# One decoder layer on one core: two tile pairs' normalisation postponed, and five scan parts moved ahead of the attention slots

## The chip, the core and the metric

The kernel runs on one NeuronCore of a Trainium2 chip. TensorE (PE) multiplies, VectorE (DVE), ScalarE (ACT) and GpSimd (POOL) work on tiles in the on-chip memory (SBUF), and SyncE (SP) issues most of the transfers from HBM. The engines run side by side and order themselves by semaphores. The metric is the device time of one execution in microseconds (us), less is better.

## What is computed

One inference step of a one-layer hybrid decoder, for 256 prompt tokens and 8 sequences of 8 new tokens: 320 token columns in all.

```
xn = rmsnorm(x, g_mix_norm);  z = xn @ w_in          # 2048 -> 5120 columns, split in q k v | u | h gb gc
o_att  = dilated window attention(q, k, v [, cached K/V of 8 sequences])
y_ssm  = glu(gelu(scan(B u) C + D u))                # diagonal complex state space, 64-dim state
y_conv = gb * conv3(gc * h)
x = x + concat(rmsnorm(o_att), rmsnorm(y_ssm), rmsnorm(y_conv)) @ w_out
x = x + (silu(xn' @ w_gate) * (xn' @ w_up)) @ w_down ; final rmsnorm       # xn' = rmsnorm(x)
```

All of it is float32. Data lie feature-major: a tile is 128 features by 320 tokens.

## The kernel before, in words

**Weights.** Each weight matrix is streamed once, in units of 256 rows by 512 columns (512 KB). To keep float32 accuracy a unit is split in two float32r halves. ACT makes `whi`, the rounded part (`high(u)`, L716), and DVE makes `wlo`, the rest (`low(u)`, L1112). The activations are split in the same way in `xh` and `xl`. PE then does three products for each of 4 output banks and 2 row tiles: whi with xh, whi with xl, wlo with xh. That is 24 matmuls of 320 columns a unit. `whi` and `wlo` have two buffers each, so `high(s+2)` waits until PE has finished unit s (`unit_done`), and `low(s+2)` waits for `high(s+2)`.

**Slots.** Units 0 to 79 are w_in, in ten groups of eight units; units 80 to 95 are the first half of w_out. In a group the first and the last unit are edge units: PE's matmuls are L2030, L2031 and L2036 there, and wlo is wanted after the first bank. The six inner units have L1990 and L1992, and wlo is wanted after all 16 whi matmuls. All engines have their side work written out by hand in the same slots s = 0 to 95. On DVE and ACT a slot has work ahead of `low(s+2)` / `high(s+2)` and work behind it; what stands behind it in slot s can start only once PE is done with unit s. On PE side work stands in the middle of a unit (`middle`) or after it (`end`).

**The norm at the start.** Groups 0 and 1 (units 0 to 15) are multiplied with the raw x times the gain, and their result is scaled by `rstd` as it is taken from the banks (`evict`, L1124). From group 2 on (unit 16) the x of the products is normalised: `normed_x(j)` (DVE, L1134, two tiles), `normed_high(j)` (ACT, L695, two tiles of xh), `normed_low(j)` (DVE, L1140, two tiles of xl). Unit 16 + j of PE uses tiles 2j and 2j+1, and its first matmul of each tile waits for that tile's xl (semaphore `r_lo`, L1988 in an inner unit). In the kernel before, `normed_x(j)` stands in slot 12 + j and `normed_low(j)` in slot 13 + j, both behind `low`.

**The scan.** The state space part has 16 steps of five parts (`scan`, L1193 to L1221; 10 DVE instructions or so each step). `SCAN_TIME` gives each slot from 24 to 64 a weight, and the 80 parts are dealt to the slots in proportion. POOL makes the tables of step i (`table`, L1714 to L1720) after step i-2 has ended; ACT makes the decays.

**Attention of the new tokens.** Eight batches start in slots 36, 42, ... 78, and last 17 slots or more. For each: `queries` on ACT (L754) in the slot before the start; scores on PE (L1835) in the four slots from the start; masks and maxima on DVE (L1152, L1171); biases and exponents on ACT (L767, L798) in slots 4 and 5; the transpose on DVE (L1182) ahead of `low` in slot 6; the values on PE (L1841) from slot 7. In slot 4, ACT's `spread_bias` waits for DVE's `maxima`.

**Later.** The prompt's attention, the gate of the state space part, its norm (`SUM_SSM` = slot 76) and the convolution's norm (`SUM_CONV` = slot 83) follow to slot 95. Then come the rest of w_out, w_gate/w_up and w_down in hardware loops; the change touches nothing of them.

Of the kernel before, what the change touches and what calls it, by code (L numbers as in the profile page):

```python
# [87 lines left out]
U_IN, U_DOWN = D_MODEL // 256, D_FF // 256  # L88
# [8 lines left out]
BT_SLOT, VN_SLOT = 18, 56  # L97

NORM_SLOT, PLAIN = 12, 2
# [8 lines left out]
SUM_SSM, SUM_CONV = 76, 83  # L108
# [104 lines left out]
def build(nc, a, o):  # L213
    with ExitStack() as ctx:
# [195 lines left out]
        SCAN_TIME = [0 if s % U_IN == U_IN - 2 else 10 if s < SCAN1 else 12 if s < SCAN2 else 19 for s in range(SCAN_END)]  # L410
# [102 lines left out]
        def released(key):  # L513
# [11 lines left out]
                    "vn": lambda: ("vn_moved", key[1] + 1),  # L525
# [144 lines left out]
        def _(act):  # L670
# [19 lines left out]
            def normed_high(j):  # L690

                for k in range(2 * j, 2 * j + 2):
                    act.wait_ge(S["x_norm"], k + 1)
                    act.wait_ge(S["unit_done"], SPL + U_IN + j + 1)
                    act.activation(xh[:, k, :], x1[:, k, :], ACT.Copy, scale=vec[:, V_MIX + k:V_MIX + k + 1]).then_inc(S["r_hi"], 1)  # L695
# [164 lines left out]
            for s in range(SLOTS):  # L860
# [26 lines left out]
                if NORM_SLOT <= s < NORM_SLOT + U_IN:  # L887
                    normed_high(s - NORM_SLOT)
# [55 lines left out]
                for b in batches(s, -1):  # L944
                    queries(b)
# [5 lines left out]
                for b in batches(s, 4):  # L951
                    spread_maxima(b)
                    spread_bias(b)
                    exponent(b, (0, 1))
                for b in batches(s, 5):
                    exponent(b, (2, 3))
# [106 lines left out]
        def _(dve):  # L1063
# [248 lines left out]
            for s in range(SLOTS):  # L1312
# [31 lines left out]
                if NORM_SLOT <= s < NORM_SLOT + U_IN:  # L1344
                    normed_x(s - NORM_SLOT)
                if NORM_SLOT < s <= NORM_SLOT + U_IN:
                    normed_low(s - NORM_SLOT - 1)
# [19 lines left out]
                if s == BT_SLOT - 3:  # L1367
                    input_matrices()
                if s == BT_SLOT - 2:
                    input_sums()  # L1370
# [40 lines left out]
                for b in batches(s, 4):  # L1411
                    maxima(b)
# [11 lines left out]
                if s == SUM_SSM:  # L1424
                    scales_first(1, rstd_s)
                if s == SUM_SSM + 1:
                    scales_rest(1, rstd_s)
                    normed(ZU, V_OUT + 12, rstd_s)
                for i, part in scan_parts(s):
                    scan(i, part)  # L1430

# [146 lines left out]
        def _(pool):  # L1578
# [118 lines left out]
            pool.wait_ge(S["bt_done"], 2)  # L1697
# [563 lines left out]
```

## Time and profile before

| | us |
|---|---|
| median of 3 runs (1516.50 to 1517.22) | 1516.99 |
| the profiled execution's own time | 1517.05 |
| its span, first to last instruction | 1515.0 |
| PE busy in the span | 1487.5 |
| DVE busy | 840.8 |
| ACT busy | 633.4 |
| POOL busy | 224.4 |

The profile's times count from the span's start. An engine that is idle before an instruction has that idle time in brackets behind it, with what ended it. Unit 16 starts at 64.02 us, unit 24 at 100.14, unit 42 at 175.19, unit 49 at 222.78, and unit 95 at 510.56.

### The profile page before, as it was taken

The page shows a single profiled execution, that of the slowest core. Times are in us where ns is not written, and L with a number is a line of the kernel's source. Part 1 is how long each engine was busy: PE and PEld are TensorE (multiplying, and loading weights), DVE is VectorE, ACT ScalarE, POOL GpSimd, SP SyncE. Part 2 cuts the span into 40 slices and gives each one's busy share as a digit, 9 for nine tenths or more (in the row PEclk, how much of TensorE's full clock was granted, in tenths as well). Part 3 has the DMA queues.
Part 4 walks back from the last instruction along what each step waited for, and adds up shares of the span by engine and source line. Part 5 has one row for each costly group of instructions (what it writes and reads, how often), then busy time and mean ns, then how long its engine had stood idle before and what let it go on. Part 6 is the DMA issues. An engine that isn't in the chain of part 4 may idle for free.

```text
span 1515.0 us, 28035 instructions
## 1 busy us (share of the span) xinstructions
PE 1487.5 (98%) x11367; PEld 1421.2 (94%) x11367; DVE 840.8 (56%) x1061; ACT 633.4 (42%) x1027; POOL 224.4 (15%) x317
## 2 busy tenths in 40 slices
PE   9989999999999999999999999999999999999997
PEld 9989877888877999999999999999999999999997
DVE  7779789983477677445444444445444433343334
ACT  6444545557666354433333333333333333234332
POOL 7874335310540000000000000000000000000100
PEclk9999999999999999999999999999999999999999
DMA  7536799999888444444444444444444444444442
GB/s 268 166 124 232 273 349 357 363 385 388 296 332 307 154 142 151 153 146 147 151 152 146 146 151 152 148 145 150 152 149 145 150 153 152 145 150 153 147 151 106
DMA packets 93271, 296.40 MB, mean 196 GB/s; under 512 B 9728, under 2 KB 11008, under 8 KB 92800
## 3 DMA queue, kind: packets, MB, share of 16 engines
q1 hardware_dynamic: 92608, 294.10, 56.9%
q8 instruction: 62, 1.02, 0.3%
q10 hardware_dynamic: 576, 1.08, 0.2%
q14 instruction: 25, 0.20, 0.0%
HBM read 289.06 MB, written 5.43 MB: 194 GB/s over the span
## 4 chain that ended last, share of the span: by engine, by line
PE 84%; DVE 8%; ACT 3%; POOL 2%; issue 2%; DMA 0%; DVEq 0%; ACTq 0%
PE ps L2147 20%; PE ps L2148 20%; PE ps L2146 20%; PE ps L1990 5%; PE ps L2030 2%; PE ps L1992 2%; PE ps L2036 2%; PE ps L2031 2%; PE ps L1835 2%; DVE wlo L1112 2%; PE ps L1841 2%; PE ps L2099 1%; PE ps L2098 1%; PE ps L2097 1%; ACT whi L716 1%
## 5 line engine op out<-in xcount | busy, mean ns | idle before, releaser
L1465 DVE TENSOR_TENSOR wlo<-raw,whi 128x1024 fp32r<-128x1024 f32 x264 | 325.2, 1232 | 519.9 <-ACT whi L989 519.8
L989 ACT ACTIVATE whi<-raw 128x1024 fp32r<-128x1024 f32 x264 | 279.9, 1060 | 606.2 <-PE ps L2148 601.7
L2148 PE MATMUL ps<-xh,wlo 128*128 128x320 f32 x1400 | 432.6, 309 | 0.0
L2146 PE MATMUL ps<-xh,whi 128*128 128x320 f32 x1400 | 432.6, 309 | 0.0
L2147 PE MATMUL ps<-xl,whi 128*128 128x320 f32 x1400 | 432.6, 309 | 0.0
L2147 PEld LDWEIGHTS ps<-xl,whi 128*128 128x128 f32 x1400 | 262.8, 188 | 0.0
L2148 PEld LDWEIGHTS ps<-xh,wlo 128*128 128x128 f32 x1400 | 262.8, 188 | 0.0
L2146 PEld LDWEIGHTS ps<-xh,whi 128*128 128x128 f32 x1400 | 262.8, 188 | 0.0
L2146 PE MATMUL ps<-hh,whi 128*128 128x320 f32 x696 | 215.1, 309 | 0.0
L2147 PE MATMUL ps<-hl,whi 128*128 128x320 f32 x696 | 215.1, 309 | 0.0
L2148 PE MATMUL ps<-hh,wlo 128*128 128x320 f32 x696 | 215.1, 309 | 0.0
L1112 DVE TENSOR_TENSOR wlo<-raw,whi 128x1024 fp32r<-128x1024 f32 x110 | 138.2, 1256 | 79.1 <-ACT whi L716 78.4
L716 ACT ACTIVATE whi<-raw 128x1024 fp32r<-128x1024 f32 x110 | 116.0, 1057 | 146.1 <-PE ps L1990 71.8
L1761 POOL TENSOR_TENSOR sq_last<-sq_last 128x1280 f32<-128x1280 f32 x2 | 5.9, 2970 | 996.2 <-ACT sq_last L675 996.2
L1990 PE MATMUL ps<-xh,whi 128*128 128x320 f32 x472 | 144.8, 320 | 2.2 <-ACT whi L716 2.2
L1992 PE MATMUL ps<-xl,whi 128*128 128x320 f32 x472 | 139.4, 309 | 0.0
L2146 PEld LDWEIGHTS ps<-hh,whi 128*128 128x128 f32 x696 | 130.7, 188 | 0.0
L2147 PEld LDWEIGHTS ps<-hl,whi 128*128 128x128 f32 x696 | 130.7, 188 | 0.0
L2148 PEld LDWEIGHTS ps<-hh,wlo 128*128 128x128 f32 x696 | 130.7, 188 | 0.0
L1990 PEld LDWEIGHTS ps<-xh,whi 128*128 128x128 f32 x472 | 88.6, 188 | 14.8 <-issue 8.1
L2030 PE MATMUL ps<-xh,whi 128*128 128x320 f32 x280 | 89.6, 328 | 4.1 <-ACT z L710 2.3
L1992 PEld LDWEIGHTS ps<-xl,whi 128*128 128x128 f32 x472 | 88.7, 188 | 0.2
(340 smaller groups left out, 1872.4 us busy)
## 6 DMA issues: line engine op xcount, KB each, us to landing
raw<-in_w_gu SPq DMA_DIRECT2D x176, 512.0 KB, 3.7
raw<-in_w_dn SPq DMA_DIRECT2D x88, 512.0 KB, 3.7
raw<-in_w_in SPq DMA_DIRECT2D x78, 512.0 KB, 5.0
kv<-in_cv SPq DMA_DIRECT2D x64, 512.0 KB, 7.2
kv<-in_ck SPq DMA_DIRECT2D x32, 768.0 KB, 6.7
kv<-in_ck SPq DMA_DIRECT2D x32, 512.0 KB, 6.9
raw<-in_w_out SPq DMA_DIRECT2D x32, 512.0 KB, 3.8
raw<-in_cv SPq DMA_DIRECT2D x16, 512.0 KB, 7.7
```

The lines of the kernel that those rows point to most:

```text
L716: act.activation(whi[:, u % SPL, :], raw[:, raw_place(u), :], ACT.Copy).then_inc(S["w_hi"], 1)
L989: act.activation(whi[:, j % SPL, :], raw[:, j % RAW, :], ACT.Copy).then_inc(S["w_hi"], 1)
L1112: v.tensor_tensor(wlo[:, u % SPL, :], raw[:, raw_place(u), :], whi[:, u % SPL, :].bitcast(F32), ALU.subtract) \
L1465: v.tensor_tensor(wlo[:, j % SPL, :], raw[:, j % RAW, :], whi[:, j % SPL, :].bitcast(F32), ALU.subtract) \
L1835: last = t_.matmul(ps[32 * j:32 * j + 32, 7, 64 * c0:64 * c1], qst[:, b % 2, 2 * i + half, :], keys[:, :, half, :, j, :], start=(half == 0 ...
L1841: last = t_.matmul(ps[32 * g:32 * g + 32, bank, 0:2 * P], turned[:, g, :], vals[:, 2 * P * g:2 * P * g + 2 * P], start=start, stop=stop, t ...
L1990: last = t_.matmul(ps[:, b0 + n, 0:NT], src[:, u % SPL, w], xh[:, k, :], start=False, stop=False)
L1992: t_.matmul(ps[:, b0 + n, 0:NT], whi[:, u % SPL, w], xl[:, k, :], start=False, stop=False)
L2030: t_.matmul(out, whi[:, u % SPL, w], xh[:, k, :], start=first, stop=False)
L2146: t_.matmul(out, whi[:, slot, w], ah[:, k, :], start=(k == 0), stop=False)
L2147: t_.matmul(out, whi[:, slot, w], al[:, k, :], start=False, stop=False)
L2148: last = t_.matmul(out, wlo[:, slot, w], ah[:, k, :], start=False, stop=(k == 2 * units - 1))
```

## The change

Pairs 2 to 7 of the normalisation stand two slots later (`NORM_AT`), and within a slot `normed_low` goes ahead of `normed_x`. The input matrices of the scan stand in slots 16 and 21 instead of 15 and 16, their transposes on PE in slot 22 instead of 18, and POOL doesn't wait for these transposes any more ahead of the scan's tables. The scan's weights are other ones: the slots from 24 to 41 get 31 of the 80 parts instead of 26, and by slot 60 both kernels are at the same part again. For each batch, ACT's queries come one slot earlier, all biases and exponents are in slot 5, and DVE's maxima stand at the end of slot 4. The convolution's norm is one slot later, and the state space norm's two halves on DVE are in one slot.

```diff
-BT_SLOT, VN_SLOT = 18, 56
-
-NORM_SLOT, PLAIN = 12, 2
+BT_MADE, BT_SUMS, BT_SLOT, VN_SLOT = 16, 21, 22, 56
+
+NORM_AT, PLAIN = (12, 13, 16, 17, 18, 19, 20, 21), 2
...
-SUM_SSM, SUM_CONV = 76, 83
+SUM_SSM, SUM_CONV = 76, 84
...
-        SCAN_TIME = [0 if s % U_IN == U_IN - 2 else 10 if s < SCAN1 else 12 if s < SCAN2 else 19 for s in range(SCAN_END)]
+        TURN_SLOTS = [first + TURN for first in START_OF]
+        SCAN_TIME = [0 if s % U_IN == U_IN - 2 else 10 if s in TURN_SLOTS else 13 if s < SCAN1 else 14 if s < SCAN2 else 19 for s in range(SCAN_END)]
...
-                if NORM_SLOT <= s < NORM_SLOT + U_IN:
-                    normed_high(s - NORM_SLOT)
+                for j in range(U_IN):
+                    if NORM_AT[j] == s:
+                        normed_high(j)
...
-                for b in batches(s, -1):
+                for b in batches(s, -2):
                     queries(b)
...
                 for b in batches(s, 4):
                     spread_maxima(b)
+                for b in batches(s, 5):
                     spread_bias(b)
-                    exponent(b, (0, 1))
-                for b in batches(s, 5):
-                    exponent(b, (2, 3))
+                    exponent(b, range(4))
...
-                if NORM_SLOT <= s < NORM_SLOT + U_IN:
-                    normed_x(s - NORM_SLOT)
-                if NORM_SLOT < s <= NORM_SLOT + U_IN:
-                    normed_low(s - NORM_SLOT - 1)
+                for j in range(U_IN):
+                    if NORM_AT[j] + 1 == s:
+                        normed_low(j)
+                for j in range(U_IN):
+                    if NORM_AT[j] == s:
+                        normed_x(j)
...
-                if s == BT_SLOT - 3:
+                if s == BT_MADE:
                     input_matrices()
-                if s == BT_SLOT - 2:
+                if s == BT_SUMS:
                     input_sums()
...
-                for b in batches(s, 4):
-                    maxima(b)
...
                 if s == SUM_SSM:
-                    scales_first(1, rstd_s)
+                    scales(1, rstd_s)
                 if s == SUM_SSM + 1:
-                    scales_rest(1, rstd_s)
                     normed(ZU, V_OUT + 12, rstd_s)
                 for i, part in scan_parts(s):
                     scan(i, part)
+                for b in batches(s, 4):
+                    maxima(b)
...
-            pool.wait_ge(S["bt_done"], 2)
```

## Rows read from the trace of the kernel before

**Rows 1.** The page: busy time of each engine, its share of the span.
```profile
PE 1487.5 (98%) x11367; PEld 1421.2 (94%) x11367; DVE 840.8 (56%) x1061; ACT 633.4 (42%) x1027; POOL 224.4 (15%) x317
```

**Rows 2.** PE's waits over the whole span: in total us, times, longest.
```profile
PE ps L2030 <- ACT z L710: 2.3, 1, 2.3
...
PE ps L1835 <- issue: 1.7, 1, 1.7
...
PE ps L1781 <- DVE sqc L1379: 1.6, 1, 1.6
...
PE ps L1835 <- ACT qst L754: 1.2, 1, 1.2
PE ps L1835 <- DVE smax L1152: 1.0, 1, 1.0
```

**Rows 3.** Stretches: PE, PEld, DVE, ACT, POOL busy (count), PE clock, DMA share, GB/s.
```profile
49.94:53.46 3.52, 3.52 (x26) 3.52 (x25) 3.40 (x5) 1.06 (x1) 3.30 (x6) 1.00 0.49 164
...
64.02:100.14 36.12, 30.53 (x203) 29.00 (x202) 32.97 (x49) 15.43 (x23) 33.31 (x52) 1.00 0.39 120
100.14:145.10 44.96, 44.47 (x306) 42.86 (x305) 36.99 (x42) 20.93 (x37) 19.49 (x20) 1.00 0.63 217
...
168.04:222.78 54.74, 50.26 (x488) 42.23 (x484) 47.44 (x76) 28.27 (x81) 18.23 (x18) 0.94 0.89 326
222.78:326.93 104.15, 104.02 (x1166) 84.02 (x1162) 98.14 (x156) 54.18 (x161) 42.85 (x42) 1.00 0.97 359
```

**Rows 4.** PE's timeline: start, us; unit 13 starts; three waits, units 16 to 22.
```profile
53.46 0.31 PE L1990 MATMUL ps<-xh,whi 128*128 128x320 f32 x1
...
67.33 0.41 PE L2030 MATMUL ps<-xh,whi 128*128 128x320 f32 x1 [1.39 <-DVE z L1124]
...
79.55 1.09 PE L1956 MATMUL ps<-ident,bmat 128*128 128x128 f32 x8 [1.99 <-DVE bmat L1241]
...
93.00 0.41 PE L1990 MATMUL ps<-xh,whi 128*128 128x320 f32 x1 [1.57 <-ACT whi L716]
```

**Rows 5.** ACT's timeline: `high(14)`, which waits for the end of unit 12.
```profile
53.72 1.06 ACT L716 ACTIVATE whi<-raw 128x1024 fp32r<-128x1024 f32 x1 [2.46 <-PE ps L1990]
```

**Rows 6.** DVE's timeline: slot 12, the evictions, the matrices' first product, the last `normed_low`.
```profile
54.88 1.23 DVE L1112 TENSOR_TENSOR wlo<-raw,whi 128x1024 fp32r<-128x1024 f32 x1 [1.37 <-ACT whi L716]
56.03 1.03 DVE L1134 TENSOR_TENSOR x<-x,rstd 128x320 f32<-128x320 f32 x2
...
66.80 2.47 DVE L1124 TENSOR_TENSOR z<-ps,rstd 128x320 f32<-128x320 f32 x6
...
72.27 0.72 DVE L1229 TENSOR_TENSOR btmp<-bmat,par 128x512 f32<-128x512 f32 x1
...
94.12 1.16 DVE L1140 SCALAR_TENSOR_TENSOR xl<-x,vec,xh 128x320 fp32r<-128x320 f32 x2
```

**Rows 7.** DVE's timeline: a scan instruction without POOL beside it; `low` and the same with.
```profile
109.14 0.48 DVE L1205 TENSOR_TENSOR tm<-tm 128x320 f32<-128x320 f32 x1
...
120.14 1.64 DVE L1112 TENSOR_TENSOR wlo<-raw,whi 128x1024 fp32r<-128x1024 f32 x1
...
122.53 1.03 DVE L1205 TENSOR_TENSOR tm<-tm 128x320 f32<-128x320 f32 x1
```

**Rows 8.** PE's timeline: unit 31 waits for wlo.
```profile
126.96 0.56 PE L2036 MATMUL ps<-xh,wlo 128*128 128x320 f32 x2 [0.49 <-DVE wlo L1112]
```

**Rows 9.** ACT's timeline in slot 46: the biases wait for DVE's maxima.
```profile
210.84 0.89 ACT L767 ACTIVATE sbias<-sbias 32x4 f32<-32x4 f32 x4 [4.32 <-DVE sbias L1171]
```

**Rows 10.** PE's timeline at the end of unit 47 and in unit 48.
```profile
209.67 1.93 PE L1841 MATMUL ps<-kv,ptk 128*32 128x256 f32 x32
213.89 0.38 PE L2030 MATMUL ps<-xh,whi 128*128 128x320 f32 x1 [2.29 <-ACT z L710]
...
215.23 0.47 PE L2031 MATMUL ps<-xl,whi 128*128 128x320 f32 x1
```

**Rows 11.** A stretch of unit 48, columns as in Rows 3.
```profile
216.00:218.00 2.00, 2.00 (x7) 0.86 (x6) 1.93 (x5) 1.85 (x9) 0.00 (x0) 0.50 1.05 376
```

More of the change, by code:

```diff
@@ L524, in released @@
                     "bt": lambda: ("bt_moved", key[1] + 1),
-                    "vn": lambda: ("vn_moved", key[1] + 1),
+                    "vn": lambda: ("vn_moved", 2),
                     "av": lambda: ("o_scaled", key[1] + 1),
```

## The prediction

> **What bounds the kernel now.** The page's busy times come first [rows 1]: PE is busy for 1487.5 of 1515.0 us, so no more than about 27 us of idle time can be won, and any new wait of PE is paid in full. PE's waits tell where the idle time lies [rows 2]: all of them are in the part with the slots, none is in the hardware loops behind it. The stretches show what stands behind the waits [rows 3]. A plain unit takes 3.52 us with no idle time, 24 matmuls at 0.147. Units 16 to 23 take 36.12 us, where eight plain units are 28.2 and the transposes of the scan's matrices about 1.1, so 6.8 us are waits; three of them are in [rows 4], and DVE is busy for 32.97 of the 36.12, so DVE is the cause. Units 24 to 35 take 44.96 us with next to no wait. Units 40 to 48 take 54.74 with some 8 us lost, partly at a lower clock.
>
> **The change, part by part.**
>
> *Pairs 2 to 7 of the norm (the term that decides).* The order in time inside a slot is what matters. When PE ends unit s (call it D), ACT starts `high(s+2)` 0.26 us later: unit 13 starts at 53.46 [rows 4] and the instruction at 53.72 [rows 5]. DVE starts `low(s+2)` at 54.88, and its next instruction, which is the first behind `low` in slot s, starts at 56.03 [rows 6], so D + 2.57. Unit 16 + j waits for the xl of pair j with its first matmul. Before, the pair is made in slot 13 + j, behind the end of unit 13 + j. PE has two more units to do until it asks for it, and the last pair, at 94.12, is done 1.3 us ahead of unit 23's start at 96.6 (100.14, where the third stretch of [rows 3] begins, less one unit). After, pairs 2 to 7 are made in slots 17 to 22, so pair j comes behind the end of unit 15 + j, and unit 16 + j is the very next one. PE can't start it before D + 2.57 + one `normed_low` instruction (half of 1.16, about 0.5, [rows 6]), so D + 3.1; the second tile comes 0.45 later where PE wants it 0.3 later, about 0.15 more. Each of units 18 to 23 therefore costs 3.52 + 0.15 + 3.1 = 6.8 us instead of 3.52. Nothing hides this: PE has no other work ahead of the unit, save the transposes of the matrices (1.1 us), which now lie in the wait ahead of unit 23 and cost nothing there.
>
> The start of that stretch: slots 14 and 15 of DVE lose two pairs (about 1 us for each `normed_x` and `normed_low`, [rows 6]), so the evictions end about 1.2 us earlier and PE's 1.39 us wait at 67.33 [rows 4] shrinks to about 0.3. Unit 17 then ends at about 71.6. But DVE is later: evictions to 68.3 (six in 2.47, [rows 6]), two `low` to 70.6, `normed_x(2)` to 71.6, and the matrices' four products, now in slot 16, at 0.7 each, to 74.3. Then `low(19)` to 75.5 and the first xl at 76.0. Unit 18 starts at 76.1, 4.5 us behind the end of unit 17. Five further periods of 6.8 put unit 23 at 110.1, and unit 24 starts at 113.7 instead of 100.14: **+13.6**. Bounds: 12.0 if the products delay nothing and each period is 0.1 shorter, 15.5 if POOL beside DVE lengthens the chain by 0.3 each time. The wait of 1.99 for the matrices [rows 4] is gone in this, since the sums in slot 21 have 3 us to spare.
>
> *POOL's wait for the transposes.* It goes, but POOL waits for all of xl too and that comes later than before; its first table needs 5 us and DVE wants it 9 us after unit 23's start. Nothing, at most 0.3 either way.
>
> *Scan parts ahead of attention.* Slots 25 to 35 now hold two parts each (but for two of them). DVE's slot is then 1.15 for `low` + 2.5 to 3.1 = 3.65 to 4.3 against a unit of 3.52 [rows 3], and instructions beside POOL's table are longer: 1.03 instead of 0.48, and 1.64 for `low` [rows 7]. At unit 31, an edge unit that wants wlo at once, PE waits already now [rows 8]. DVE falls about 2 us further behind there and again ahead of unit 39. I take +2.7 over units 24 to 39; bounds 0 (DVE may be one unit late without a wait) and +5.
>
> *ACT's order in slots 4 and 5, and the queries.* In slot 46 ACT stood for 4.32 us before the biases, waiting for DVE's maxima [rows 9]. Behind them stood unit 47's evictions and `high(49)`, so PE waited 2.29 [rows 10], and then PE ran at half its clock: 0.50 granted (1.2 GHz) [rows 11], so 320 columns take 0.267 instead of 0.147, and one matmul 0.47 from start to end instead of 0.31 [rows 4, 10]; about 3.4 us are lost in unit 48. After, ACT is free here. The queries' 1.2 and about 0.7 of the 1.0 for the mask [rows 2] go too. That is 2.3 + 3.4 + 1.9 = 7.6. But what is late next is near: DVE is busy for 47.44 of the 54.74 us, and DMA's share is 0.89 in the mean [rows 3] and 1.05 at unit 48 [rows 11]. The same bytes in 8 us less would ask for 380 GB/s over the whole stretch. I take -5.4, bounds -8.1 and -2. In units 49 to 65, where PE has no wait worth naming now, the missing 8 us of slack are only half made up by the parts that went, and I add +1.0 (0 to +3).
>
> *Slots 70 to 78.* Four exponents and the biases in one slot make ACT 2.8 us later at slot 72, which is full of table loads: +0.8. In slot 76 the norm's reciprocal and the rest of it stand in a row, but the maxima no longer stand before them, and slot 77 has 1.5 us less ahead of the prompt's masks, which hold the bank for which PE's scores of slot 78 waited (1.7, the wait put down to issue in [rows 2]): -1.5. Together -0.7, bounds -2.6 and +1.5.
>
> *The convolution's norm one slot later.* PE's wait of 1.6 for the sum [rows 2] goes, but the reciprocal now stands ahead of unit 85's eviction, and unit 86 waits some 0.7 longer: -1.0, bounds -1.7 and +1.5.
>
> **The sum**, against the profiled execution's own time of 1517.05 (span 1515.0 and 2.05 around it): 13.6 + 2.7 - 5.4 + 1.0 - 0.7 - 1.0 = +10.2, so 1527.3. The median shown, 1516.99, is 0.06 lower, which changes nothing.
>
> **Rivals.**
>
> *The clock falls in the new waits.* It fell once, behind 1.93 us of narrow matmuls and 2.29 us of idleness [rows 10, 11]; it did not fall at 79.55 behind 1.99 us of idleness nor at 93.00 [rows 4]. The new waits are 3.1 us each with a full unit between them, the first 4.5, so longer than any of these. Each unit at half clock takes 24 x 0.267 = 6.4 us instead of 3.5: 2.9 more, since the wait behind it starts only at its end. One such unit is within my range; three of six give 1527.3 + 8.7 = 1536. The Trainium skill, TensorE: Matmul & The Clock Gate, section "HAM oscillation — how this bites in real kernels", says that a stream of short bursts of matmuls with waits between them lets the clock fall again at every wait, which speaks for this rival; by that rule all six units would be slow and the sum 17 us larger. The row for unit 48 shows the fall, the rows for units 18 and 22 show waits without one.
>
> *DVE is the bound in more places.* Moving parts ahead makes it late in 24 to 39 by the upper bound, and units 49 to 65 stand on their upper bound: +5.0 - 2.7 and +3 - 1, and attention gives 2 back instead of 5.4. 1527.3 + 2.3 + 2.0 + 3.4 = 1535.
>
> *It evens out.* All waits behind unit 24 in the slots, some 11.3 us with those of [rows 2], and the 3.4 of the clock go without a new one, and the norm costs 12.0: 1517.05 + 12.0 - 14.7 = 1514.4, with half a wait left 1517. For it: each of them has a cause that the change touches. Against it: DVE's 98.14 of 104.15 us in units 49 to 65, with DMA at 0.97 [rows 3], leave no room for all.
>
> *Faster: the xl is there in time.* If DVE got to `normed_low(j)` before PE ended unit 15 + j, the 6.8 us of waits in units 16 to 23 would go instead of growing, and with attention's 5.4 the time is 1517.05 - 6.8 - 5.4 = 1505. It decides at one point, whether `low(s+2)` really waits for unit s. All starts of `high` that I read stand 0.26 behind a unit's end or later [rows 5], so I give it little.
>
> **How the numbers follow.** Forecast 1527.3 (its own range 1522 to 1533): 0.62. Clock 0.16, DVE 0.08, evens out 0.08, faster 0.04, something else that is slower 0.02. About 0.2% (3 us) is what a measurement of this kernel tells from no change. Faster by more: the last rival and a tail of the third, 0.05. Within: the rest of the third, 0.07. Slower: 0.88. The range for 8 in 10 leaves out the third and fourth rival and the far half of the first: 1520 to 1537. The Trainium skill, SBUF — State Buffer, section "Who interferes with whom", says that a DVE instruction with two SBUF inputs is blocked by a GpSimd instruction that reads SBUF for its whole length. [Rows 7] agree (1.03 for 0.48); by that rule scan parts dealt more densely meet POOL's tables just as often as before, so the +2.7 would be at its lower half.
>
> **What would show it.** Right: in the changed kernel's timeline each of units 18 to 23 starts right behind an xl instruction of L1140 or its like, DVE's `low` is directly ahead of it, starts lie 6.8 us apart, unit 24 at 113 to 114; ACT has no 4 us wait before the biases; the scores of slot 42 don't wait for queries; the clock stays at 1.00 at unit 48. Wrong: unit 24 starts before 105; the clock's fall shows in 76 to 114; units 24 to 39 take under 68 us (no DVE overload) or over 73; units 40 to 48 take over 52 us.

## The result: 24 us slower, and where they are in the profile

The changed kernel takes 1541.29 us (median of 4 executions, 1541.02 to 1544.48), the kernel before beside it 1516.74 (1516.18 to 1517.22): 1.0167 times as long, 95% interval 1.0149 to 1.0184. The forecast was 1527.3 with a range to 1537. So the sign was right and the size was not: +24.5 us measured, +10.2 forecast. The profiled execution took 1541.31 with a span of 1539.5. (The title says two tile pairs; it is six, pairs 2 to 7, that are postponed, by two slots each.)

The page gives the busy times, to be read beside [rows 1]. PE has the same 11,367 matmuls and is busy for 6.9 us more. Most of that is the clock: in the stretches below PE works for 18.2 us at half clock, in the kernel before for 6.83 us (the row of it below), and half of the difference is 5.7. The other 17.6 us of the longer span are idle time.

```profile
PE 1494.4 (97%) x11367; PEld 1427.8 (93%) x11367; DVE 839.2 (55%) x1061; ACT 632.9 (41%) x1025; POOL 217.7 (14%) x317
```

```profile
214.68:221.51 6.83, 6.83 (x25) 5.35 (x23) 6.00 (x10) 3.88 (x12) 0.00 (x0) 0.50 1.02 378
```

PE's waits of the changed kernel, columns as in [rows 2]. The waits for `xl` are new; those for `wlo` grew; the one for `sp` is in unit 77. In this kernel the lines are one further down (L1141 is `normed_low`, L1113 `low`, L717 `high`).

```profile
PE ps L1991 <- DVE xl L1141: 17.0, 6, 4.1
PE ps L2037 <- DVE wlo L1113: 4.0, 3, 2.6
PE ps L1889 <- DVE sp L1270: 2.2, 1, 2.2
PE ps L2031 <- DVE xl L1141: 2.1, 1, 2.1
```

PE's timeline says where they are. Units 18 to 23 begin with these instructions, against [rows 4], which had three waits in the same stretch. The starts are 8.59, 8.89, 9.39, 8.25 and 6.87 us apart; only the last distance, which has no half clock in it, is near the 6.8 of the forecast.

```profile
76.58 0.61 PE L1991 MATMUL ps<-xh,whi 128*128 128x320 f32 x1 [4.08 <-DVE xl L1141]
85.17 0.38 PE L1991 MATMUL ps<-xh,whi 128*128 128x320 f32 x1 [3.57 <-DVE xl L1141]
...
94.06 0.61 PE L1991 MATMUL ps<-xh,whi 128*128 128x320 f32 x1 [3.02 <-DVE xl L1141]
103.45 0.60 PE L1991 MATMUL ps<-xh,whi 128*128 128x320 f32 x1 [3.02 <-DVE xl L1141]
111.70 0.39 PE L1991 MATMUL ps<-xh,whi 128*128 128x320 f32 x1 [3.02 <-DVE xl L1141]
118.57 0.38 PE L2031 MATMUL ps<-xh,whi 128*128 128x320 f32 x1 [2.15 <-DVE xl L1141]
```

DVE's timeline shows why: the pair's `xl` stands directly behind `low`, and `low` behind ACT's `high`, which waits for the end of the unit just done. At 84.13, beside POOL, the two instructions take 1.83 instead of 1.01.

```profile
82.79 1.42 DVE L1113 TENSOR_TENSOR wlo<-raw,whi 128x1024 fp32r<-128x1024 f32 x1 [4.94 <-ACT whi L717]
84.13 1.83 DVE L1141 SCALAR_TENSOR_TENSOR xl<-x,vec,xh 128x320 fp32r<-128x320 f32 x2
...
92.23 1.22 DVE L1113 TENSOR_TENSOR wlo<-raw,whi 128x1024 fp32r<-128x1024 f32 x1 [4.76 <-ACT whi L717]
93.37 1.01 DVE L1141 SCALAR_TENSOR_TENSOR xl<-x,vec,xh 128x320 fp32r<-128x320 f32 x2
```

Stretches of the changed kernel, columns as in [rows 3]. The first four lie in units 18 to 21, each wholly at a granted clock of 0.50 (1.2 GHz); the sixth, in unit 32, is at 0.50 too. The last four are compared with [rows 3] below.

```profile
76.00:79.30 3.30, 2.72 (x10) 2.75 (x11) 1.85 (x4) 1.02 (x2) 3.07 (x10) 0.50 0.46 159
86.30:89.60 3.30, 3.30 (x14) 3.30 (x14) 1.17 (x2) 1.12 (x2) 2.67 (x5) 0.50 0.21 81
93.10:99.80 6.70, 5.74 (x22) 5.77 (x22) 2.08 (x5) 1.02 (x2) 0.00 (x0) 0.50 0.23 78
103.30:106.60 3.30, 3.15 (x12) 3.18 (x13) 1.27 (x4) 1.01 (x2) 0.00 (x0) 0.50 0.49 159
...
151.44:157.80 6.36, 3.80 (x25) 3.54 (x25) 6.26 (x7) 2.88 (x6) 5.13 (x6) 1.00 0.66 231
157.95:161.25 3.30, 3.30 (x13) 3.30 (x14) 2.37 (x3) 0.00 (x0) 0.00 (x0) 0.50 0.74 227
196.74:244.94 48.20, 48.19 (x505) 40.44 (x501) 43.59 (x74) 28.55 (x81) 17.20 (x19) 1.00 0.92 338
244.94:349.61 104.67, 102.83 (x1150) 83.40 (x1146) 92.66 (x148) 52.22 (x152) 37.94 (x36) 1.00 1.00 374
...
122.28:196.74 74.46, 68.90 (x570) 63.36 (x568) 63.23 (x78) 32.35 (x63) 36.01 (x38) 0.98 0.59 200
349.61:535.10 185.49, 178.48 (x1770) 149.07 (x1767) 112.33 (x268) 116.42 (x307) 36.31 (x50) 1.00 0.84 311
```

In the first four PE is busy for 14.91 us at half clock; at the full clock the same work would take half of that, so by this estimate some 7.5 us are the clock's. Set against the stretches of before:

| stretch | before, us | after, us | difference | forecast |
|---|---|---|---|---|
| up to the start of unit 24 | 100.14 | 122.28 | +22.1 | +13.6 |
| units 24 to 39 | 67.90 | 74.46 | +6.6 | +2.7 |
| units 40 to 48 | 54.74 | 48.20 | -6.5 | -5.4 |
| units 49 to 65 | 104.15 | 104.67 | +0.5 | +1.0 |
| units 66 to 94 | 183.63 | 185.49 | +1.9 | -1.7 |

PE waits as forecast in the first row, but its clock falls too. In the second, units 31 and 32 wait for `wlo`, and the clock falls behind the longer wait:

```profile
151.44 0.56 PE L2037 MATMUL ps<-xh,wlo 128*128 128x320 f32 x2 [1.20 <-DVE wlo L1113]
157.78 0.83 PE L2037 MATMUL ps<-xh,wlo 128*128 128x320 f32 x2 [2.56 <-DVE wlo L1113]
```

### The profile page after: what moved, and what is told of

The parts are those of the page before. It is cut to its first block, busy times and chain, and to the rows that moved or that the text cites. A ratio compares the mean times of both kernels' runs of the same rounds, so it can differ in the third digit from the quotient of the medians.

```text
span 1539.5 us, 28026 instructions
## 1 busy us (share of the span) xinstructions
PE 1494.4 (97%) x11367; PEld 1427.8 (93%) x11367; DVE 839.2 (55%) x1061; ACT 632.9 (41%) x1025; POOL 217.7 (14%) x317
## 4 chain that ended last, share of the span: by engine, by line
PE 85%; DVE 7%; ACT 3%; POOL 2%; issue 2%; DMA 0%; DVEq 0%; ACTq 0%
PE ps L2148 20%; PE ps L2147 20%; PE ps L2149 20%; PE ps L1991 6%; PE ps L1993 3%; PE ps L2031 2%; PE ps L1836 2%; PE ps L2037 2%; PE ps L2032 2%; DVE wlo L1113 2%; PE ps L1842 2%; ACT whi L717 1%; PE ps L2099 1%; PE ps L2100 1%; PE ps L2098 1%
## 5 line engine op out<-in xcount | busy, mean ns | idle before, releaser
L2147 PEld LDWEIGHTS ps<-xh,whi 128*128 128x128 f32 x1400 | 263.0, 188 | 0.0
L2148 PEld LDWEIGHTS ps<-xl,whi 128*128 128x128 f32 x1400 | 263.0, 188 | 0.0
L1113 DVE TENSOR_TENSOR wlo<-raw,whi 128x1024 fp32r<-128x1024 f32 x110 | 138.4, 1259 | 97.3 <-ACT whi L717 96.5
L717 ACT ACTIVATE whi<-raw 128x1024 fp32r<-128x1024 f32 x110 | 116.3, 1057 | 174.8 <-PE ps L1991 85.3
L1991 PEld LDWEIGHTS ps<-xh,whi 128*128 128x128 f32 x472 | 92.4, 196 | 31.8 <-issue 28.1
L1993 PEld LDWEIGHTS ps<-xl,whi 128*128 128x128 f32 x472 | 92.5, 196 | 0.2
```

Source lines behind the costliest of these rows:

```text
L717: act.activation(whi[:, u % SPL, :], raw[:, raw_place(u), :], ACT.Copy).then_inc(S["w_hi"], 1)
L1113: v.tensor_tensor(wlo[:, u % SPL, :], raw[:, raw_place(u), :], whi[:, u % SPL, :].bitcast(F32), ALU.subtract) \
L1991: last = t_.matmul(ps[:, b0 + n, 0:NT], src[:, u % SPL, w], xh[:, k, :], start=False, stop=False)
L1993: t_.matmul(ps[:, b0 + n, 0:NT], whi[:, u % SPL, w], xl[:, k, :], start=False, stop=False)
L2147: t_.matmul(out, whi[:, slot, w], ah[:, k, :], start=(k == 0), stop=False)
L2148: t_.matmul(out, whi[:, slot, w], al[:, k, :], start=False, stop=False)
```

## The experiments

Ratios are to runs of the kernel before on the same chip, and the number in brackets behind a ratio is its 95% interval. Each was run in at least three rounds. "Unit 24" is its start, 100.14 before and 122.28 after. One more line of the change, not in the diff ahead, lets the bank of the transposed values be used again only when both halves are moved (`"vn": lambda: ("vn_moved", 2)`). The kernels below with the scan's weights, the attention's order or all but the norm have it too; it was not tried by itself.

### The norm alone, and all the rest alone

The first is the kernel before with the norm's part (in the diff: `NORM_AT`, `BT_MADE`, `BT_SUMS`, `BT_SLOT`, the loops over `NORM_AT`, POOL's wait). The second is the changed kernel with that part undone.

```diff
-NORM_SLOT, PLAIN = 12, 2
+NORM_AT, PLAIN = (12, 13, 16, 17, 18, 19, 20, 21), 2
```

> The kernel before with the norm's part of the change alone (pairs 2 to 7 two slots later, normed_low ahead of normed_x, the scan's matrices in slots 16, 21 and 22, POOL's wait gone). My theory, that each of units 18 to 23 waits for its own xl behind the end of the unit before it and that the clock falls in these waits: unit 24 starts about 22 us later than in the kernel before, and from there the time is the old one, so 1516.7 + 22 = 1539, at least 1535. Rival, that the norm's part costs only the 13.6 us of waits that I forecast and the rest of the changed kernel's loss comes from the moved scan and attention work: 1530.

> The changed kernel with the norm's part undone: what is left is the scan's weights, ACT's and DVE's order for the batches, and the two later norms. My theory, that the remainder is worth what the changed kernel's trace shows behind unit 24 (+6.6 us in units 24 to 39, -6.5 in 40 to 48, +2.4 behind): 1516.7 + 2.4 = 1519, between 1516 and 1522. Rival, that the losses in units 24 to 39 are an echo of the late norm and go with it: 1512 to 1514, faster than before.

Measured: the norm alone 1539.53 us (1537.13 to 1540.35), ratio 1.0152 [1.0135, 1.0169]; unit 24 at 121.09. The rest alone 1518.81 (1517.33 to 1520.52), ratio 1.0011 [1.0002, 1.0021]. So the norm's part is nearly the whole loss, and these two parts add: +22.6 and +1.9 against +24.5 for both. Its stretches at half clock lie elsewhere than in the full change, but are there too (PE busy for 12.02 of the 13.4 us):

```profile
78.10:81.50 3.40, 3.40 (x15) 3.40 (x14) 0.04 (x1) 0.64 (x2) 3.17 (x11) 0.50 0.27 102
85.00:91.70 6.70, 5.56 (x21) 5.55 (x22) 3.38 (x5) 1.12 (x2) 3.98 (x7) 0.50 0.25 78
95.20:98.50 3.30, 3.06 (x11) 3.09 (x12) 1.36 (x4) 1.02 (x2) 0.00 (x0) 0.50 0.46 159
```

### The clock kept up in the waits

The changed kernel with matmuls that nobody reads, in a free bank, behind units 17 to 22, so that PE works where it would wait.

```diff
+WARM = {17: 28, 18: 20, 19: 20, 20: 20, 21: 20, 22: 12}
...
+                if s in WARM:
+                    if s == 17:
+                        pe.wait_ge(S["z_done"], 8)
+                    for n in range(WARM[s]):
+                        t_.matmul(ps[:, 5, 0:NT], xh[:, 0, 0:P], xh[:, 0, :], start=True, stop=True)
```

> The changed kernel with PE busy in its waits: behind units 17 to 22 it does 28, 20, 20, 20, 20 and 12 matmuls of 320 columns into a bank that nobody uses then (their results are not read). If the 7.4 us by which units 18 to 21 are longer than work plus wait are the clock's, the granted clock is 1.00 up to unit 24, each unit's period is 6.8 us, unit 24 starts near 114.5 and the time is about 1534. If they are something else (wlo late, contention), the time stays at 1541 or is longer by what the extra matmuls add.

Measured: 1535.53 (1535.26 to 1537.05), ratio 1.0127 [1.011, 1.0144]. Unit 24 starts at 115.79, 6.5 us earlier than in the change, and the clock stays at 1.00 from unit 17 to there; it still falls in unit 32:

```profile
68.47:115.79 47.32, 45.90 (x303) 43.72 (x301) 27.84 (x43) 14.86 (x22) 22.69 (x46) 1.00 0.29 92
...
151.45:154.75 3.30, 3.30 (x13) 3.30 (x14) 2.37 (x3) 0.00 (x0) 0.00 (x0) 0.50 0.62 197
```

So of the +22.1, 6.5 hang on the clock alone, and 15.65 are what the order of the work costs at full clock. The filling itself costs little: units 20 to 22 take 6.9 us each here, and in the norm alone, where nothing is filled in, units 21 and 22 take 6.88 each at full clock. The forecast was 13.6 with an upper bound of 15.5.

### One slot later instead of two

The changed kernel with each of pairs 2 to 7 one slot earlier.

```diff
-NORM_AT, PLAIN = (12, 13, 16, 17, 18, 19, 20, 21), 2
+NORM_AT, PLAIN = (12, 13, 15, 16, 17, 18, 19, 20), 2
```

> The changed kernel with pairs 2 to 7 one slot later than before instead of two: (12, 13, 15, 16, ... 20). If the point from which the wait decides is whether normed_low(j) stands behind the end of unit 14+j or 15+j, the xl is ready 0.4 us ahead of its unit here: no wait above 0.6 us in units 19 to 23, clock 1.00, unit 24 starts within 3 us of the kernel before's 100.1, and the time is 1516 to 1522. If merely being later costs in proportion to the slots, half of the 22 us stay: 1530.

Measured: 1528.26 (1527.73 to 1529.56), ratio 1.0079 [1.0062, 1.0096], unit 24 at 107.76. The expectation failed: the slot that I had counted as enough still costs 7.6 us. (The time is near the rival's 1530, a cost in proportion to the slots; the next kernels show that it is not that.) The timelines of DVE and ACT show a ring that I had not seen:

```profile
92.72 0.89 DVE L1135 TENSOR_TENSOR x<-x,rstd 128x320 f32<-128x320 f32 x2
95.24 1.23 DVE L1113 TENSOR_TENSOR wlo<-raw,whi 128x1024 fp32r<-128x1024 f32 x1 [1.63 <-ACT whi L717]
96.38 1.01 DVE L1141 SCALAR_TENSOR_TENSOR xl<-x,vec,xh 128x320 fp32r<-128x320 f32 x2
...
99.83 1.23 DVE L1113 TENSOR_TENSOR wlo<-raw,whi 128x1024 fp32r<-128x1024 f32 x1 [1.63 <-ACT whi L717]
```

```profile
93.24 1.02 ACT L696 ACTIVATE xh<-x,vec 128x320 fp32r<-128x320 f32 x2 [2.62 <-DVE x L1135]
94.17 1.04 ACT L717 ACTIVATE whi<-raw 128x1024 fp32r<-128x1024 f32 x1
```

DVE makes `xl`, then `x`; ACT's `xh` waits for `x`; ACT's `high`, which waits for nothing itself, stands behind `xh`; DVE's next `low` waits for it. One round takes 4.59 us (95.24 to 99.83), against 3.52 for a unit. The Trainium skill, Perfetto Trace Analysis, section "Tensor Engine Instruction (MATMUL, LD_WEIGHTS)", says that ACT and DVE run strictly in order; ACT's rows agree. Not all of the 7.6 us are waits for `xl`. In unit 22 PE also waits for the sums of the scan's matrices, which stand behind that slot's `low` and `xl`:

```profile
103.31 1.09 PE L1957 MATMUL ps<-ident,bmat 128*128 128x128 f32 x8 [2.37 <-DVE bmat L1242]
```

That the ring is the cause was only argued from these rows, so the next two kernels tried it.

### The ring broken, with one slot and with two

Both have ACT's `normed_high` one slot behind `normed_x`, so that it never stands ahead of a `high` that could run. The first has the pairs one slot later and the matrices in slots 15, 20 and 22, so their products and sums one slot earlier than in the kernel just shown. The second has two slots and the change's places; it differs from the kernel with the norm alone by the line below and nothing else.

```diff
-                    if NORM_AT[j] == s:
+                    if NORM_AT[j] + 1 == s:
                         normed_high(j)
```

> The kernel before with another placing of the norm: pairs 2 to 7 one slot later than before instead of two (slots 15 to 20), normed_low ahead of normed_x, and ACT's normed_high of a pair one slot behind its normed_x, so behind the next high(s+2) and not ahead of it. The input matrices in 15, 20, transposes 22. With normed_high in the same slot the same placing lost 7.6 us by unit 24; the cause I named is a ring through both engines: low, normed_low, normed_x, ACT's normed_high, then the next high and low, 4.58 us round. If that is the cause, the ring is broken here: unit 24 at 97 to 102 us (before 100.1), no wait over 1 us in units 18 to 21, time 1513 to 1519. If the lateness is of DVE's amount of work or of the one slot itself, waits of 1 to 2 us stay at units 18 to 22, unit 24 is at 105 or later, and the time is 1522 to 1529.

> The change's norm with its two slots' delay, the change's other places and order, but ACT's normed_high one slot behind normed_x. With one slot's delay this took the whole loss away (unit 24 at 99.9 instead of 107.8). My theory of the norm: with two slots it is DVE's low ahead of the pair's xl that holds PE, not the ring through ACT. It expects the waits of 3 to 4 us ahead of units 18 to 23 unchanged, unit 24 at 113 to 122 and 1529 to 1540. If the ring through ACT was the cause here too, unit 24 is at 108 or earlier and the time is 1524 or less.

Measured with one slot: 1516.66 (1515.79 to 1517.48), ratio 1.0002 [0.9992, 1.0011], unit 24 at 99.92. The 7.6 us are gone. From unit 19 to unit 22, where no work on the matrices stands on DVE's way, the three units take 12.42 us here and 16.16 with one slot and the ring; so at least these 3.7 us were the ring's. For the rest, the 2.37 us wait for the sums above all, the ring and the matrices' slot are not told apart, since both were changed here. ACT now has `xh` behind `whi` without a wait:

```profile
83.02 1.06 ACT L716 ACTIVATE whi<-raw 128x1024 fp32r<-128x1024 f32 x1 [1.55 <-PE ps L1992]
83.99 1.01 ACT L695 ACTIVATE xh<-x,vec 128x320 fp32r<-128x320 f32 x2
```

One thing that I expected is not so: unit 18 still waits, for longer than 1 us, and has half a clock in its stretch. Units 17 and 19 start 2.0 and 1.2 us earlier than in the kernel before, so it costs nothing by unit 24.

```profile
74.30 0.61 PE L1992 MATMUL ps<-xh,whi 128*128 128x320 f32 x1 [3.47 <-DVE xl L1141]
```

Measured with two slots: 1538.93 (1537.07 to 1539.71), ratio 1.0143 [1.0127, 1.0158], unit 24 at 123.57, just over my 113 to 122. The norm alone, with the ring, has 1539.53. PE's last four waits are those of the change to the hundredth, two of them here:

```profile
95.05 0.61 PE L1992 MATMUL ps<-xh,whi 128*128 128x320 f32 x1 [3.02 <-DVE xl L1141]
...
111.55 0.56 PE L1992 MATMUL ps<-xh,whi 128*128 128x320 f32 x1 [3.02 <-DVE xl L1141]
```

So two mechanisms lie one behind the other: with one slot the ring holds PE, with two it is not the ring, and mending it gives nothing. That it is then the order on DVE, `xl` behind `low`, is what its rows show; a kernel with `xl` ahead of `low` was not tried.

### The scan's weights alone

```diff
-        SCAN_TIME = [0 if s % U_IN == U_IN - 2 else 10 if s < SCAN1 else 12 if s < SCAN2 else 19 for s in range(SCAN_END)]
+        TURN_SLOTS = [first + TURN for first in START_OF]
+        SCAN_TIME = [0 if s % U_IN == U_IN - 2 else 10 if s in TURN_SLOTS else 13 if s < SCAN1 else 14 if s < SCAN2 else 19 for s in range(SCAN_END)]
```

> The kernel before with the new SCAN_TIME alone (and with the release of the bank for the transposed values put off until both are moved, as in the change; it is needed by the new order and costs at most one wait of tenths of a us at slot 56). My theory of units 24 to 39: the scan parts are the whole cause of the loss there. It expects unit 24 at 100.1 as before, unit 40 some 5.5 to 6.5 us later than before, with a wait of 2 to 3 us for wlo at unit 32 and one fall of the clock to half behind it (3.4 us at 0.50), unit 42 to 48 no more than 1.5 us shorter than before, since ACT's order in slots 4 and 5 is the old one, and 1519 to 1523 us in all. The rival, that the parts only bring forward what DVE would be late with at attention, expects the loss to be given back by unit 49 (DVE's maxima come earlier there since the scan's parts are fewer), and 1515 to 1518.

Measured: 1524.47 (1521.74 to 1525.35), ratio 1.0055 [1.0039, 1.0072]; unit 40 comes 4.7 us later than before. The two waits for `wlo` are those of the change, but in this execution the clock did not fall behind them:

```profile
128.95 0.57 PE L2037 MATMUL ps<-xh,wlo 128*128 128x320 f32 x2 [1.19 <-DVE wlo L1113]
135.29 0.56 PE L2037 MATMUL ps<-xh,wlo 128*128 128x320 f32 x2 [2.54 <-DVE wlo L1113]
```

```profile
126.90:138.30 11.40, 7.66 (x48) 7.13 (x49) 10.78 (x12) 4.16 (x9) 6.29 (x6) 1.00 0.69 244
```

DVE is busy for 10.78 of the 11.40 us: it is the bound there. My figures of 5.5 to 6.5 us and of a fall were too much for this execution. But it is the fastest of the four, 1521.74, and the others took 1523.61 to 1525.35; the median is above my 1519 to 1523. Units 42 to 48 became 3.4 us shorter, where I had allowed 1.5, so at unit 49 only 2.25 of the lateness is left, as the rival said. But the cause is at least in part another: the half clock of unit 48 is missing in this execution, and it is missing in another one too whose code up to there is the old one (below, `SUM_CONV` alone). Then 2.7 us are lost again, so unit 66 is 4.9 late. This happens behind unit 55, at a wait for DVE's maxima with half a clock behind it:

```profile
266.30 1.56 PE L1836 MATMUL ps<-kv,qst 128*32 128x192 f32 x32 [2.42 <-DVE smax L1153]
```

### The attention's order alone

The kernel before with the three edits to queries, exponents and maxima.

```diff
-                for b in batches(s, -1):
+                for b in batches(s, -2):
...
                 for b in batches(s, 4):
                     spread_maxima(b)
+                for b in batches(s, 5):
                     spread_bias(b)
-                    exponent(b, (0, 1))
-                for b in batches(s, 5):
-                    exponent(b, (2, 3))
+                    exponent(b, range(4))
```

> The kernel before with the attention's part of the change alone: queries a slot earlier, the biases and exponents in slot 5, DVE's maxima at the end of slot 4 (and the bank's release as in the change). The scan's weights are the old ones. My theory: the 7.5 us that units 40 to 48 give back come from ACT's freed order, not from the scan's parts that went. It expects unit 24 and 40 as before, unit 49 some 6 to 7.5 us earlier, clock 1.00 at unit 48, and 1509 to 1512 us. The rival, that the parts had to go from the attention's slots for DVE to keep up, expects the maxima behind more scan work in slot 46 and with them ACT later, half of the gain or less by unit 49, and 1513 to 1517.

Measured: 1514.25 (1513.91 to 1516.02), ratio 0.9989 [0.9979, 0.9998]. The stretch of units 40 to 48 is as short as in the change, with the scan's old weights; so the gain there needs the attention's order alone, and no scan part had to move for it. About half of it is a fall of the clock that the kernel before has in its profile and not in every execution (the last section has the rows). The next stretch, units 49 to 65, takes 105.76 instead of 104.15:

```profile
168.34:216.84 48.50, 47.10 (x489) 39.89 (x485) 46.11 (x74) 28.65 (x81) 18.32 (x18) 1.00 0.91 333
216.84:322.60 105.76, 104.18 (x1167) 84.00 (x1163) 101.10 (x159) 53.18 (x156) 41.74 (x42) 1.00 0.99 370
```

The total missed my 1509 to 1512 and lies in the rival's range, though not for its reason: of 6.2 us won there, 3.4 are given back behind unit 49, 1.9 of them behind unit 85. There, ahead of unit 86, PE waits 2.37 (before, 0.5), put down to "issue". DVE stands for 2.75 us (before, 0.83) for ACT's four exponents ahead of the transpose, and `low` and the evictions of unit 85's banks come behind that:

```profile
470.80 0.38 PE L2029 MATMUL ps<-xh,whi 128*128 128x320 f32 x1 [2.37 <-issue]
```

```profile
465.57 1.65 DVE L1181 STREAM_TRANSPOSE ptk<-sall 128x1408 f32<-128x1408 f32 x1 [2.75 <-ACT sall L798]
```

### The new order for six of the eight batches

The kernel with the attention's order alone, but with batches 5 and 7 (starts 66 and 78) as they were. The diff is against that kernel.

```diff
+OLD = (5, 7)
...
                 for b in batches(s, 4):
                     spread_maxima(b)
+                    if b in OLD:
+                        spread_bias(b)
+                        exponent(b, (0, 1))
                 for b in batches(s, 5):
-                    spread_bias(b)
-                    exponent(b, range(4))
+                    if b in OLD:
+                        exponent(b, (2, 3))
+                    else:
+                        spread_bias(b)
+                        exponent(b, range(4))
...
+                for b in batches(s, 4):
+                    if b in OLD:
+                        maxima(b)
...
                 for b in batches(s, 4):
-                    maxima(b)
+                    if b not in OLD:
+                        maxima(b)
```

> The attention's part of the change alone, but for batches 5 and 7 (starts 66 and 78) in the old order: their biases and first exponents in slot 4, their maxima where they were. With all eight batches in the new order 5.9 us were won by unit 49 and 3.8 of them given back: 1.15 at unit 52, 0.5 at 55, 0.96 at 73 (a wait for the gated y) and 1.9 at 85, where four exponents and the biases in slot 83 kept ACT from high(85) and DVE's transpose behind the norm's table load. My theory: the last two come from the two batches named. It expects unit 73 without the 1.2 us wait, unit 85 with 0.5 instead of 2.4, and 1510.5 to 1512. The rival, that any work brought forward shows up as the same wait elsewhere behind unit 66, expects unit 95 within 0.7 us of the version with all eight, 1513.5 to 1515.

> The same, and the norm as in the kernel with normed_high one slot behind normed_x and pairs 2 to 7 one slot late. Alone that placing gave nothing by unit 42, and 1.5 us at unit 48 where the clock was half for 3.4 instead of 6.8 us. My theory: with the attention's part in place there is no fall of the clock at unit 48 to be shortened, so it is within 1 us of the kernel without it: 1510 to 1512.5. The rival, that the 1.0 us won ahead of unit 18 comes through when nothing else falls, expects 1509 to 1510.

Measured: 1511.12 (1511.02 to 1512.48), ratio 0.9965 [0.9952, 0.9979], the fastest kernel of the study, 5.5 us faster than before. The waits behind unit 85 and in unit 73 are back at 0.45 and 0.40 (before, 0.45 and 0.31; with all eight batches, 2.37 and 1.27), so they did come from batches 7 and 5. With the norm placed anew as well: 1511.80 (1511.26 to 1512.84), ratio 0.997 [0.9958, 0.9981], so nothing more, as expected. The page of the first, for [rows 1]: PE is busy for 3.3 us less than in the profile before; in this execution the clock is at 1.00 in all of the slots.

```profile
PE 1484.2 (98%) x11367; PEld 1418.8 (94%) x11367; DVE 842.7 (56%) x1061; ACT 634.6 (42%) x1027; POOL 223.3 (15%) x317
```

### The late norms alone

The first kernel has both edits, the second only `SUM_CONV`.

```diff
-SUM_SSM, SUM_CONV = 76, 83
+SUM_SSM, SUM_CONV = 76, 84
...
-                    scales_first(1, rstd_s)
+                    scales(1, rstd_s)
                 if s == SUM_SSM + 1:
-                    scales_rest(1, rstd_s)
```

> The kernel before with the convolution's norm one slot later and the state space norm's two halves in one slot, nothing else. My theory now: these two edits are worth nothing as a pair. PE's wait of 1.6 at unit 83 goes, waits for the gated y come in units 85 to 87 (some 2 us together), and at units 76 to 78 +1.5 and -1.7 cancel: the time is 1516 to 1518. The rival, the sum as I forecast it (about -1 here and -1.5 at 76), expects 1514 to 1515.

> The kernel before with the convolution's norm one slot later, and nothing else: with both of the late edits, 5.3 us were lost, +1.8 at units 77 and 78 and +3.9 from 83 on (the wait of 1.6 left unit 83 and came as 2.2 in unit 84 with half a clock behind it, then 1.0 and 1.4 at units 85 and 87). My theory: the two parts are independent. It expects units 76 to 82 as before, the same +3 to +4 from 83 to 88, and 1519 to 1520.5. The rival, that the loss behind 83 is only the clock that had fallen before, expects 1516 to 1518.

Measured: both 1521.85 (1519.27 to 1522.78), ratio 1.003 [1.0019, 1.0041]; `SUM_CONV` alone 1519.65 (1518.65 to 1521.45), ratio 1.0021 [1.0012, 1.003]. My expectation for the pair, nothing, fell, and so did its rival, a gain. The pair costs 1.5 us in units 76 to 78, where the forecast gain of 1.5 did not come. That 1.5 is about what the clock costs there, behind a wait of 2.43 for `sp`: PE works for 3.30 us at half clock in unit 78.

```profile
423.30:426.60 3.30, 3.30 (x16) 2.90 (x16) 2.08 (x5) 2.20 (x10) 2.93 (x5) 0.50 0.99 376
```

In the changed kernel, which waits 2.17 at the same place and has the full clock behind it, the same three units gain 0.3. And in each profile PE's wait for the convolution's sum has only moved one unit on, and grown: 1.6 in [rows 2] against this row of the pair and 1.98 with `SUM_CONV` alone:

```profile
467.32 1.13 PE L1780 MATMUL ps<-sqc,ones 128*128 128x320 f32 x2 [1.99 <-DVE sqc L1379]
```

Units 83 to 87 take 4.4 us longer with the pair, which met half a clock there, and 2.8 with `SUM_CONV` alone, which did not. So the clock is no more than 1.6 of it, and the order costs 2.8, a little under the 3 to 4 that I gave. What stands ahead of unit 83 adds only 0.4: this execution lacks the half clock of unit 48 (2.9 us earlier at unit 49) and loses 3.5 us at unit 52, by a wait of 1.91 with half a clock behind it.

The eight executions of the pair fall in two groups, three of 1519.3 to 1519.9 us with a granted clock of 0.996 over the whole, and five of 1521.8 to 1522.8 with 0.994 or 0.995; the profile is of the second. So of the median's +5.5 some 2.4 hang on whether the clock falls.

## Why the prediction was wrong in size and right in mechanism

**The norm: mechanism right, price too low by two terms.** Each of units 18 to 23 waits for an `xl` behind `low`, as forecast, and the test with two slots and no ring shows that it is not ACT that holds PE. The sum took 13.6; the kernel with the clock kept up gives 15.65 for the same order. Of the 2.05 between them, 0.7 are in the start of unit 18 (76.82 against my 76.1), and 1.3 in the five periods, of which two are long, 7.36 and 7.25. In the first of these DVE works beside POOL (at that place in the change, 1.83 for 1.01), which I had as a bound of 0.3 a period but not in the sum. The step that failed is the next one: I priced six waits of some 3 us (measured, 2.15 to 4.08) without their effect on the clock and put that effect into a rival with a chance of 0.16. It cost 6.5 us by the kernel with filled waits, 7.5 by the rows at half clock. The rival priced it at 8.7, with 1536 in all; the rest of the 1541.29 is in the other terms. The rows that I read as evidence against it, waits of 1.99 and 1.57 at full clock [rows 4], were shorter than the new ones; only the fall behind 2.29 [rows 10, 11] was near them, and I should have gone by it. By what the prediction cites of the Trainium skill, TensorE: Matmul & The Clock Gate, section "HAM oscillation — how this bites in real kernels", all six units would have been slow and the cost 17; the trace shows four stretches and 7.5, so it agrees in the sign and not in the size.

**Units 24 to 39: right place, too small, and the clock again.** DVE is late at unit 31 and more so at 32. The scan's weights alone cost 4.7 without a fall of the clock, at the upper end of my 0 to 5 where I took 2.7; that the denser parts would meet POOL's tables no more often, and so stay at the lower half, did not come true. Of the other 1.9 in the change, some 1.65 are a fall behind the 2.56 us wait (3.30 us of PE work at half clock in the sixth stretch); my bounds had no clock in them.

**Units 40 to 48: right, in part by luck.** -6.5 against -5.4. The attention alone gives -6.2 there, ACT stands no more for the maxima, and the clock is at 1.00. But 3.4 us of my sum were the fall at unit 48, and whether that fall comes differs between executions: without it the old code takes 51.69 us here (last section), and the new order is 3.2 us shorter than that.

**Units 49 to 65: right in size.** +0.5 against +1.0.

**Units 66 to 94: wrong sign.** Units 70 to 78 were to give -0.7 and cost +0.7: the wait for the gated y at unit 73 costs 1.0 as allowed for, but units 76 to 78 gain 0.3 instead of 1.5, since PE now waits for `sp` ahead of the masks of unit 77. Units 83 to 87 were to give -1.0 and cost +1.2. PE's wait for the convolution's sum did shrink, from 1.56 to 0.41, and the one ahead of unit 86 grew by 0.8, as I had it. What I had not is a new wait ahead of unit 88, which the kernels with the late norms have as well:

```profile
507.25 0.38 PE L2031 MATMUL ps<-xh,whi 128*128 128x320 f32 x1 [1.34 <-ACT whi L717]
```

**What the miss is made of.** The time came 14.3 us over the forecast: 8.5 of it up to unit 24 (6.5 the clock, 2.05 the order), 3.9 in units 24 to 39, 3.6 behind unit 66, less 1.6 in units 40 to 65. Two of the signs of being wrong that the prediction names were there: half a clock between 76 and 114, and over 73 us for units 24 to 39.

**The four parts do not add.** The norm and all the rest together do, but split further, alone they measure +22.6 (norm), +8.1 (scan), -2.1 (attention) and +5.5 (late norms), together 34, against 24.5. A good part of that is which executions had a fall of the clock. In the profiles the four are +20.28, +4.87, -2.49 and +5.67 at the start of unit 95, together 28.3 (the profiled executions of the norm and of the scan were the fastest of four). The profiles also show where the parts meet. In units 83 to 87 the attention alone costs 1.9 and the late norms 4.4, but the change only 1.2: the late exponents and the later norm fit each other, and PE's wait for the sum is 0.4 there. In units 49 to 65 the scan's weights cost 2.7, of which some 1.6 are the half clock behind that wait of 2.42, and the attention 1.6, the change 0.5. Why the last two share so much was not tried.

## What to carry to other kernels

When a wait is added ahead of a unit of matmuls, price it twice, once as the wait and once as the work behind it at half clock, and take the second into the sum where the new wait is as long as one behind which the trace shows a fall. A producer moved by whole slots should be placed by the engine's own queue: ask what stands ahead of it in that slot and what that waits for, also across a second engine, as in the ring of 4.59 us. Moving a producer and its consumer by the same slot can move the wait instead of removing it: alone, the late convolution's norm turned 1.6 us into 2.0 one unit on. And where the clock falls in some executions only, compare several executions, and take a term that rests on one fall in one profile as a chance.

## What the runs showed of the hardware

**The same wait, with a fall of the clock and without.** Of the change's three waits of 3.02 us two had half a clock behind them, of the same three in the norm alone one, and with two slots and no ring all three. At unit 32 a wait of 2.56 was followed by half a clock, and one of 2.54 with the scan's weights alone was not. The wait of 2.29 at unit 48 has half a clock behind it before [rows 10, 11]; with `SUM_CONV` alone, whose code up to there is the same, it is 2.28 and the full clock is behind it. Units 40 to 48 then take 51.69 us instead of 54.74:

```profile
168.21:219.90 51.69, 47.21 (x488) 39.90 (x484) 44.53 (x73) 28.16 (x81) 18.23 (x18) 1.00 0.89 325
```

And the wait of 1.99 for the matrices, which has the full clock behind it in the kernel before [rows 4], had half of it in three kernels whose code up to there is the same as before (the scan's weights, the attention's order, `SUM_CONV` alone); this is the stretch behind it with the scan's weights alone:

```profile
79.50:82.80 3.30, 3.30 (x14) 3.30 (x15) 3.30 (x5) 1.52 (x3) 3.14 (x6) 0.50 0.34 89
```

It cost nothing: unit 22 starts at 92.95, as before, since the later wait of 1.57 [rows 4] shrank to 0.24. So a place that shows the full clock in one profile is weak evidence for the next execution, and this fall cost nothing since PE would have waited behind it anyway.
